# Longer runs for the shifted copies of a depthwise convolution, the w_out loads moved behind the second set of copies, and smaller edits beside them

## The reference, cut to what matters

```python
h = _rmsnorm(x, norm_mix_g)
a_val, a_gate, b_gate, c_gate, b_in = split(h @ w_in)        # 5 x 512 columns
u  = a_val * sigmoid(a_gate)
ua = causal depthwise conv, width 31 (u)                     # the convolution of this case
ya = silu(head_layernorm(ua + b_conv_a)) * beta_a
z  = c_gate * b_in
yb = b_gate * causal depthwise conv, width 3 (z) * beta_b
x = x + concat(ya, yb) @ w_out
h = _rmsnorm(x, norm_ffn_g)
up = h @ w_up                                                # 2 x 2816 columns
upc = causal depthwise conv, width 3 (up)
x = x + (silu(gate half of upc) * value half of upc) @ w_down
y = _rmsnorm(x, norm_final_g)
```

## Time and profile before

| | us |
|---|---|
| median of 3 runs | 801.19 |
| lowest and highest run | 798.91, 915.09 |
| the profiled execution | 799.11 |
| its span, slowest core (7) | 797.6 |
| spans of the other cores | 793.1 to 795.5 |

### The profile page before, as it was taken

One profiled execution on the slowest core, in us unless ns is written; L12 is line 12 of the kernel. 1 busy time (PEld: TensorE's weight loads), 2 busy tenths in 40 slices (PEclk: granted clock), 3 DMA queues, 4 the chain that ended last, 5 costly groups with the idle time before them and its releaser, 6 DMA issues.

```text
span 797.6 us, 15231 instructions; the slowest of 8 cores (793.1 to 797.6 us)
## 1 busy us (share of the span) xinstructions
PE 770.9 (97%) x5048; PEld 404.1 (51%) x5048; DVE 559.5 (70%) x633; ACT 411.8 (52%) x651; POOL 213.3 (27%) x281
## 2 busy tenths in 40 slices
PE   5998999999999999999999999999999999999996
PEld 3665556555565644445444445445445444444443
DVE  4555597867686887789999999999999805233323
ACT  5455778595856567555555555555556403111112
POOL 7002021103141401354434434434434400000000
PEclk9999999999999999999999999999999999999999
DMA  8999742633685862321311322312212454532211
GB/s 180 166 219 188 204 154 90 176 133 82 172 183 176 161 191 111 47 46 31 59 32 31 58 33 33 57 32 37 52 29 45 90 163 116 201 106 106 83 73 57
DMA packets 40324, 83.82 MB, mean 105 GB/s; under 512 B 10131, under 2 KB 22931, under 8 KB 40102
## 3 DMA queue, kind: packets, MB, share of 16 engines
q1 hardware_dynamic: 32324, 53.59, 22.7%
q0 software_dynamic: 7488, 28.84, 21.1%
q10 hardware_dynamic: 434, 0.42, 0.2%
HBM read 80.90 MB, written 19.71 MB: 126 GB/s over the span
## 4 chain that ended last, share of the span: by engine, by line
PE 89%; DVE 3%; issue 3%; ACT 2%; DMA 2%; POOL 1%; DVEq 0%; ACTq 0%; POOLq 0%
PE ps L1103 37%; PE ps L1311 19%; PE ps L678 18%; PE ps L846 6%; PE ps L733 3%; PE ps L1143 3%; ACT arena L502 2%; DMA arena<-xp 2%; PE ps L646 1%; PE ps L1335 1%; DVE arena L506 1%; DVE arena L518 1%; DVE arena L511 1%; PE ps L748 1%; PE ps L755 1%
## 5 line engine op out<-in xcount | busy, mean ns | idle before, releaser
L1103 PE MATMUL ps<-arena 128*128 128x512 bf16 x1408 | 308.5, 378 | 0.7 <-ACT arena L502 0.4
L502 ACT ACTIVATE arena<-arena 128x168 f32<-128x168 f32 (+8 forms) x222 | 155.1, 704 | 234.4 <-DVE arena L511 132.3
L506 DVE SCALAR_TENSOR_TENSOR arena<-ps,arena 128x1020 f32<-128x1020 f32 (+2 forms) x200 | 234.4, 1191 | 17.8 <-ACT arena L502 9.0
L1103 PEld LDWEIGHTS ps<-arena 128*128 128x128 bf16 x1408 | 135.0, 97 | 163.2 <-issue 1.4
L506 DVE SCALAR_TENSOR_TENSOR arena<-arena 128x168 f32<-128x168 f32 (+11 forms) x217 | 187.6, 871 | 36.8 <-POOL arena L800 17.7
L678 PE MATMUL ps<-arena 128*128 128x384 bf16 (+1 forms) x960 | 158.6, 323 | 7.2 <-ACT arena L502 4.1
L1311 PE MATMUL ps<-arena 128*128 128x512 bf16 x704 | 152.1, 379 | 0.0
L511 POOL TENSOR_TENSOR arena<-arena 128x1020 bf16<-128x1020 f32 (+2 forms) x88 | 118.1, 1343 | 112.9 <-DVE arena L506 86.9
L502 ACT ACTIVATE arena<-ps,arena 128x1020 f32<-128x1020 f32 (+2 forms) x112 | 109.4, 986 | 52.4 <-PE ps L1103 51.2
L511 DVE TENSOR_TENSOR arena<-ps,arena 128x512 f32<-128x512 f32 (+4 forms) x99 | 60.9, 618 | 93.5 <-PE ps L1311 81.9
L678 PEld LDWEIGHTS ps<-arena 128*128 128x128 bf16 x960 | 92.1, 99 | 64.9 <-issue 13.6
(11 more groups left out here) (47 smaller groups left out, 249.5 us busy)
## 6 DMA issues: line engine op xcount, KB each, us to landing
arena<-xp SPq DMA_DIRECT2D x26, 512.0 KB, 7.0
arena<-wup POOLq DMA_DIRECT2D x22, 512.0 KB, 7.0
x2d<-arena SPq DMA_DIRECT2D x17, 512.0 KB, 3.2
arena<-x2d SPq DMA_DIRECT2D x17, 512.0 KB, 6.2
yp<-arena SPq DMA_DIRECT2D x15, 512.0 KB, 2.7
arena<-arena SPq DMA_DIRECT2D x64, 97.8 KB, 2.3
arena<-wdn POOLq DMA_DIRECT2D x11, 512.0 KB, 5.4
arena<-xp POOLq DMA_DIRECT2D x6, 512.0 KB, 21.8
```

The source lines that it names most:

```text
L502: P.add("act", lambda e: e.activation(out=out, in_=in_, func=func, **kw), reads=reads, writes=writes, after=after, c=c - 60.0, table=TABLE ...
L506: P.add("dve", lambda e: e.scalar_tensor_tensor(out=out, in0=in0, scalar=scalar, in1=in1, op0=op0, op1=op1), reads=reads, writes=writes, c ...
L1103: ins = e.matmul(ps[:, b, :], lhsT=wv[:, k, 128 * gv:128 * gv + 128], rhs=h2T[:, k, c0:c0 + 512], start=(k == 0), stop=(k == 7))
```

## The change

- `spread`: each transfer takes 32 partitions and one run of 4 x 416 columns (3328 bytes) from the flat buffer, shifted by 8s, padding between the channel blocks included; `ub` gets 24 columns more at its end, `U4` and `U4b` rows of 416 columns in the order (q, c). It is the same for every chunk, chunk 0 too. `conv` reads `U[:, q, c, m:m+n]`, the same numbers.
- The planner's cost of such a copy goes from 820 to 450 ns, its bytes from 4 to 2 an element.
- `w_out`'s four loads are written behind `spread(1)` and wait for the last copy of chunk 1 (`V4_33`); `xo` of chunk 0, `gb2` and `zs_h` wait for that too.
- Chunk 1's `root` is called for each tile, not once for three.
- `T1` of chunks 0 and 1 copies from PSUM on VectorE.
- `junk` becomes the last 128 columns of each of `h2T`'s 8 blocks (the sample tile's place), since U4 grows.

```diff
-        ub.append(A.bf16(o, 4 * UW).rearrange("p (c n) -> p c n", c=4))
+        ubf.append(A.bf16(o, UF))
+        ub.append(ubf[n][:, 0:4 * UW].rearrange("p (c n) -> p c n", c=4))
...
-    U4 = A.bf16(o, 16 * U4W).rearrange("p (g n) -> p g n", g=16)
+    U4 = A.bf16(o, 16 * UW).rearrange("p (q c n) -> p q c n", q=4, c=4)
...
+    U4b = h2T[:, 3:7, 0:4 * UW].rearrange("p q (c n) -> p q c n", c=4)
+    junk = h2T[:, :, H2W - 128:H2W]
...
-        nb = out.shape[0] * fsz(out) * 4
+        nb = out.shape[0] * fsz(out) * (2 if pool == "u4" else 4)
...
-                     dma=f"{pool}{i % n}", c=600.0 if eng == "pool" else (820.0 if pool == "u4" else 450.0), nbytes=nb, name=f"dma {pool}")
+                     dma=f"{pool}{i % n}", c=600.0 if eng == "pool" else 450.0, nbytes=nb, name=f"dma {pool}")
...
-        act(out, pv[:, :, 0:nt], AF.Copy, [f"ps{b}"], [okey])
+        if dve:
+            cp("dve", out, pv[:, :, 0:nt], [f"ps{b}"], [okey])
+        else:
+            act(out, pv[:, :, 0:nt], AF.Copy, [f"ps{b}"], [okey])
...
-        trans(hn_of[(1, i, t)], nt, hT[i % 2][:, :, col:col + nt], f"hT{i % 2}_{t}")
+        trans(hn_of[(1, i, t)], nt, hT[i % 2][:, :, col:col + nt], f"hT{i % 2}_{t}", dve=(i < 2))
...
-        n = CHUNKS[i][1] + 7
         p = i % 2
...
-                dma("sp", U[32 * s:32 * s + 32, q:16:4, 0:n], ub[p][32 * q:32 * q + 32, :, 8 * s:8 * s + n],
+                dma("sp", U[32 * s:32 * s + 32, q].rearrange("p c n -> p (c n)"), ubf[p][32 * q:32 * q + 32, 8 * s:8 * s + 4 * UW],
...
-        dma("sp", xo[s][0:nt, :], x_src(kind, row, nt), writes=[f"xo{s}"], pool=f"xo{s}_", n=1, after=["U4_33"])
+        dma("sp", xo[s][0:nt, :], x_src(kind, row, nt), writes=[f"xo{s}"], pool=f"xo{s}_", n=1, after=["V4_33" if i == 0 else "U4_33"])
...
     for t in range(3):
         sq1(1, t)
-    root(st1, 0, 3, "st1")
+        root(st1, t, t + 1, "st1")
...
     spread(0)
-    for q in range(4):
-        dma("pool", w_out[:, 2 * q:2 * q + 2, :].rearrange("p k n -> p (k n)"), wout[q], writes=[f"wo{q}"], pool="wo", n=4,
-            after=["U4_33"])
...
         spread(i + 1)
+        if i == 0:
+            for q in range(4):
+                dma("pool", w_out[:, 2 * q:2 * q + 2, :].rearrange("p k n -> p (k n)"), wout[q], writes=[f"wo{q}"], pool="wo", n=4,
+                    after=["V4_33"])
```

More of the change, by code:

```diff
@@ L335, in build @@
     UW = 30 + CW + 2
+    UF = 4 * UW + 24
+    ubf = []
     ub = []
     for n in range(2):
-        o = A.take(4 * UW * 2)
-        ub.append(A.bf16(o, 4 * UW).rearrange("p (c n) -> p c n", c=4))
-        A.reg(0, o, 4 * UW * 2, f"ubh{n}", *[f"ub{n}_{c}" for c in range(4)])
-    U4W = CW + 8
-    o = A.take(16 * U4W * 2)
-    U4 = A.bf16(o, 16 * U4W).rearrange("p (g n) -> p g n", g=16)
+        o = A.take(UF * 2)
+        ubf.append(A.bf16(o, UF))
+        ub.append(ubf[n][:, 0:4 * UW].rearrange("p (c n) -> p c n", c=4))
+        A.reg(0, o, UF * 2, f"ubh{n}", *[f"ub{n}_{c}" for c in range(4)])
+    o = A.take(16 * UW * 2)
+    U4 = A.bf16(o, 16 * UW).rearrange("p (q c n) -> p q c n", q=4, c=4)
     U4K = [f"U4_{s}{q}" for s in range(4) for q in range(4)]
-    A.reg(0, o, 16 * U4W * 2, *U4K)
+    A.reg(0, o, 16 * UW * 2, *U4K)
     o = A.take(128 * 32 * 2)
@@ L401, in build @@
         A.reg(0, o, 4096, f"xo{n}")
-    o = A.take(2048)
-    junk = A.bf16(o, D)
-    A.reg(0, o, 2048, "junk")
     s1_end = A.off
@@ L466, in build @@
     P.over = A.overlays()
-    xe = [A.f32(o_h2 + 4096 * n, D) for n in range(3)]
-    U4b = A.bf16(o_h2 + 12288, 16 * U4W).rearrange("p (g n) -> p g n", g=16)
+    xe = [A.f32(o_h2 + 2 * H2W * n, D) for n in range(3)]
+    U4b = h2T[:, 3:7, 0:4 * UW].rearrange("p q (c n) -> p q c n", c=4)
+    junk = h2T[:, :, H2W - 128:H2W]
     V4K = [f"V4_{s}{q}" for s in range(4) for q in range(4)]
-    assert 12288 + 32 * U4W <= 16 * H2W
+    assert 2 * D <= H2W - 128 and 4 * UW <= H2W - 128
     if debug:
@@ L557, in build @@
         for t in range(len(ch[2])):
-            P.over[f"h2_{i_}_{t}"] = ["xe0", "xe1", "xe2"] + V4K
+            P.over[f"h2_{i_}_{t}"] = ["xe0", "xe1", "xe2"] + V4K + (["junk"] if ch[2][t][0] == "s" else [])
     memset("dve", ident_f, 0.0, ["ident_f"])
@@ L562, in build @@
     for n in range(2):
-        memset("pool", ub[n], 0.0, [f"ubh{n}"] + [f"ub{n}_{c}" for c in range(4)])
+        memset("pool", ubf[n], 0.0, [f"ubh{n}"] + [f"ub{n}_{c}" for c in range(4)])
     memset("pool", zb, 0.0, ["zh"] + [f"z{c}" for c in range(4)])
@@ L620, in sq1 @@
         ap, key = xn_slot[(i, t)]
-        act(junk[0:nt, :], ap[0:nt, :], AF.Square, [key, "st1"], ["junk", f"st1_{t}"], accum_out=st1[0:nt, t:t + 1])
+        act(junk[0:nt], ap[0:nt, :].rearrange("p (k n) -> p k n", k=8), AF.Square, [key, "st1"], ["junk", f"st1_{t}"], accum_out=st1[0:nt, t:t + 1])
     def root(st, t0, t1, key):
@@ L637, in hn1, with trans @@
                 [key, f"st1_{t}", "gb1"], [f"hn{h}"])
-    def trans(h, nt, out, okey):
+    def trans(h, nt, out, okey, dve=False):
         b = st_bank()
@@ L733, in f @@
                     ins = e.matmul(ps[32 * q:32 * q + 32, b, 0:n], lhsT=L[:, 32 * c + 8 * q + m, :],
-                                   rhs=U[:, 4 * c + q, m:m + n], start=(m == 0), stop=(m == 7), skip_group_check=True)
+                                   rhs=U[:, q, c, m:m + n], start=(m == 0), stop=(m == 7), skip_group_check=True)
             if last:
@@ L859, in sq2 @@
         s = xo_slot[(i, t)]
-        act(junk[0:nt, :], xo[s][0:nt, :], AF.Square, [f"xo{s}", "st2"], ["junk", f"st2_{t}"], accum_out=st2[0:nt, t:t + 1])
+        act(junk[0:nt], xo[s][0:nt, :].rearrange("p (k n) -> p k n", k=8), AF.Square, [f"xo{s}", "st2"], ["junk", f"st2_{t}"], accum_out=st2[0:nt, t:t + 1])
     def hn2(i, t):
@@ L945, in build @@
         if i == 1:
-            dma("sp", gb2, bass.AP(g2.tensor, 0, [[0, 128], [1, D]]), writes=["gb2"], pool="c", after=["U4_33"])
-            dma("sp", zs_h.rearrange("p c s n -> p (c s n)"), zsh, writes=["zs_h"], pool="c", after=["U4_33"])
+            dma("sp", gb2, bass.AP(g2.tensor, 0, [[0, 128], [1, D]]), writes=["gb2"], pool="c", after=["V4_33"])
+            dma("sp", zs_h.rearrange("p c s n -> p (c s n)"), zsh, writes=["zs_h"], pool="c", after=["V4_33"])
             load_xo(0, 1)
```

## The result

The changed kernel takes 806.8 us (median; 806.12 to 808.75), the kernel before 799.69 beside it: ratio 1.0092, interval 1.0075 to 1.011, so 6 to 9 us slower. That is within 2%, outside the predicted 792.5 to 806, and on the other side of the forecast of 798.5.

A forecast was written before the change was run, and what follows sets the result against it. TensorE was taken as the bound, with 7.15 us of idle from 16 to 112 us to win. 799.1, -0.2 + 0.2 (chunk 1's front, T1), +1.5 (bulk arrivals), -2.1 (core 7's waits), order 0: 798.5; range 792.5 to 806.

The forecast's parts named there:

- Rival B: TensorE's waits at 50 to 53 us: long packets delay chunk 2's x and wB3, 3.5 plus 2.9 us; 803.4, chance 0.22.
- the shift of the bulk arrivals: Chunk 2's x and wB3, and TensorE behind them, come 1.5 us later (0 to 3.5) because of chunk 0's copies.
- The lower bound: Zero shift of the bulk loads: 46 packets a us with copies between them, 45 without any.
- my own upper reasoning: Most of chunk 0's 5.4 us of copies falls before x and wB3, against 1.1 before: up to 4.3, taken as 3.5.
- The 170 ns: Engine time taken for one 3328-byte copy packet, between 169 ns from 4096-byte loads and 196 ns in proportion to bytes.
- my 46 ns: Engine time taken for one small copy packet before the change, from the rates at 70 to 78 us.
- Wrong if over 250 ns: Sign that the prediction is wrong: copies of 3328 bytes taking over 250 ns a packet.
- hidden anyway: Rival: copies shorten or not, the "issue" wait on TensorE at 65.7 us stays; 799.1, chance 0.13.
- The issue: SyncE's issue falls from 0.68 us a copy to 0.33 to 0.45, 5 to 7 us for a chunk.
- 1 to 3 us later: nothing: w_out leaves 1 to 3 us after 62.00, is first read in chunk 1's last part, and costs nothing.
- rival D: GpSimd or SyncE stands at the wait for `V4_33` and a chain behind it gets late: +2 us, 801, chance 0.05.
- core 7's 3.05 us: TensorE's "issue" wait at 65.7 us on core 7, expected gone; worth -2.1, as the next core counts 795.5.

The follow-up runs named there:

- 1662-byte runs: The changed kernel, its planned order kept, with chunk 0's copies as 64 runs of 1662 bytes a transfer: 803.12 us, ratio 1.0064.
- the 830-byte kernel: The changed kernel, its planned order kept, with chunk 0's copies as 128 runs of 830 bytes a transfer: 803.75 us, ratio 1.0084.
- the one with 558: The changed kernel, its planned order kept, with chunk 0's 16 copies back in 128 runs of 558 bytes: 801.08 us, ratio 1.0051.

## Why the prediction was wrong, and where it was right

**Where the 7.3 us went** (0.0092 x 799). First by the traces of before and after, in the means of the eight cores: the span grew by 9.1 us. TensorE stands still 4.6 us longer near 50 us, 1.0 from 62 to 112 us (where the 1.2 of the 16 waits lie) and 0.7 from 112 to 640, and the half clock costs 2.7 where it cost 0.5: 8.5 together. Then by taking single edits out or putting them in. Long runs in chunk 0: 3.3 us in the changed kernel (1.0092 - 1.0051), 6.3 in the order of before. The 16 waits: 1.3 (1.0092 - 1.0076). The w_out move: 3.7 alone. They don't add up. In after TensorE is already late by the idle and the half clock near 55 us, and w_out, leaving at 71.7, is there when it comes. Take that lag away, as the kernel with chunk 0 short does, and the wait behind ScalarE near 75 us comes out, for x of chunk 3; take away the new order too, and the wait for w_out does. Rival B had the mechanism, its place and its sign, at 803.4, with a chance of 0.22.

**The step that failed first: the shift of the bulk arrivals.** I put it at 1.5 us between bounds of 0 and 3.5; x's last tile came 4.7 us later in the mean of the cores (3.8 on core 3), wB3 3.6, and TensorE stood still 4.6 us longer. That is over the upper bound too. The lower bound was the rate with small packets, which is free indeed: 30 ns beside 230. Then I took the middle although the one known thing about the new packets was that they are 4 to 6 times longer, and my own upper reasoning (their whole engine time falls before x and wB3 are in) had nothing against it but that row. The row was evidence on short packets only.

**The price of a packet.** The 170 ns came from a load out of HBM, another kind of transfer, and was yet nearly right where it mattered. From 42 to 50 us 0.82 MB are 246 packets of 3328 bytes, 0.362 x 128 / 246 = 188 ns each; before, 0.26 MB are 466 packets of 558 bytes, 0.120 x 128 / 466 = 33 ns. What was wrong is the comparison. For chunk 0 it is 512 x 188 / 16 = 6.0 us of all engines against 2048 x 33 / 16 = 4.2, where I had 5.4 against 5.9: my 46 ns was for 782 bytes, and chunk 0 carries its padding now, 1.70 MB instead of 1.14. And 6.0 less the 1.1 used before is 4.9 us, near the 4.7 that came. Here are the copies with the engines to themselves, SyncE's queue, first before (core 7, 62 to 66 us), then after (core 6, 62 to 70):

```profile
q1 hardware_dynamic: 918, 0.64, 114.5%
```

```profile
q1 hardware_dynamic: 646, 1.44, 88.1%
```

1.44 MB are 433 packets of 3328 bytes, 0.881 x 128 / 433 = 260 ns each, and 180 GB/s against 160: runs 4 times longer move the bytes at least 12% faster. At least, since the short copies fill the engines (114.5%) and the long ones don't (88.1%), and land 2.3 us after their issue: SyncE's issue may set their pace, which no run tests. "Wrong if over 250 ns" stood in the prediction; alone they are over it, beside the bulk loads not. The rule of the Trainium skill, DMA: Bandwidth & Descriptors, section Why small descriptors are slow (HBM only), that such copies are not penalized for small descriptors, is nearly what these rates show. I had cited it and let it count only for "hidden anyway"; read on, it leaves the long form no engine time to save, and none was.

**The effect on TensorE.** Rival B had 3.5 us of shift plus 2.9 for the half clock, from an idle of 2.6 us on. Measured 4.6 us more idle in the mean, and 2.7 for the clock, 3.5 on the slowest core: 1.1 and 0.6 above its. The forecast had nothing for the clock. Yet 1.25 us of waiting was there already, and with my own shift of 1.5 that makes 2.75, past the 2.61 after which core 3 ran cold before. By my own numbers the cold stretch belonged into the likeliest case. (2.61 us is no threshold: with 1662-byte runs 2.53 us was followed by half clock on core 5, and 3.20 and 3.28 were not on cores 3 and 6.)

**The issue.** Predicted 0.33 to 0.45 us a copy, 5 to 7 for 16. One takes 0.54 (0.585 for the short), 16 take 10.47 (10.87). The load of x with its 0.33 was again the row of another kind of transfer. So chunk 0's copies landed at 58.0, not by 53, and chunk 1's at 71, not 65.

**w_out "1 to 3 us later: nothing".** It left 7 to 10 us later alone, 9.7 in after, and cost 3.7 alone, with `xo`, `gb2` and `zs_h` moved too. The lateness followed from the issue price; that it had no slack I had not looked up at all, only named its first reader. GpSimd stood in front of it for 2.0 to 5.2 us in after and 7.0 to 11.2 with chunk 0 short, rival D's place; what that alone cost no run shows.

**The 16 semaphore waits** were no term of the sum: 1.3 us in after, 2.1 in the kernel before with chunk 0 short and long runs behind it.

**T1 on VectorE** takes 0.68 us, not 1.2; the low bound of 0.7 was right, and it changes nothing. (The Trainium skill, VectorE: DVE Perf Modes, section Why PSUM operands drop a tier, allows 16-bit operands out of PSUM twice the rate; 0.68 us for 1024 columns beside 0.69 for 512 of float32 agrees.)

**Right:** TensorE and the loads up to 55 us as the bound; turns one to one (371 to 368); 9,216 fewer packets in SyncE's queue (32,324 to 23,108); the root per tile and T1 winning nothing that the times can tell; core 7's 3.05 us gone; no gaps of note after 112 us; a loss or gain over 2% nearly excluded.

**Open:** what the order planned with the new costs is worth by itself. It has ScalarE's wait for x of chunk 3, and TensorE's idle from 112 to 250 us is 2.3 to 2.4 us in every kernel planned so, 1.8 in before and 1.45 in the changed kernel planned with the old costs; but no run has it without the w_out move. Also why the 830-byte kernel waits longer there than the one with 558, and why idles of one length differ in what follows (with 1662-byte runs 3.28 us before half clock on core 2, and before full clock on core 6).

## What to carry to other kernels

Where two DMA queues take turns, ask of each edit what it does to the one that gates: a long packet in the secondary queue buys its own queue speed with the other's bytes. Price a transfer by rows of its own kind (SBUF to SBUF, its number of partitions), or leave its bound as wide as not knowing is. And when a chosen value lies at the edge of a step, as 1.25 + 1.5 us of idle here beside the 2.61 that had gone cold, the step belongs in the forecast.

## What the hardware showed that I had not expected

- A wait for a semaphore that has long been raised costs TensorE's queue 0.105 us; 16 in a row 1.7 us.
- SyncE needs 0.54 us to issue a copy with 32 runs of 3328 bytes and 0.585 for one with 128 of 782: four times fewer runs save 8%.
- The same 3328-byte packet takes 188 ns where it alternates with bulk loads, and 260 ns where the copies run alone (the time of the semaphore writes counted in, both times).
- After 4.85 to 7.20 us of idle TensorE ran its next 8 matmuls at 1.2 GHz on all eight cores, and on five of them part of the 32 behind these too (5.93 to 7.00 us where 4.24 is usual), though the longest idle, 7.20, was among the other three.
